# Level 64 of the first layer's cosine and sine tables: made on POOL behind its parameters, where it stood on VectorE behind the second value unit

## What is computed

```python
def hybrid_mixer(xn, ...):
    proj = xn @ w_in
    q, k, v, u_ssm, h_conv, b_gate, c_gate, gate_logits = jnp.split(proj, IN_SPLITS, axis=-1)
    y_a = stick_breaking_attention(q, k, v) @ w_br_a
    y_b = s5_ssm(u_ssm, lam_re, lam_im, log_dt, ...) @ w_br_b
    y_c = short_conv(h_conv, b_gate, c_gate, conv_w) @ w_br_c
    g = jax.nn.sigmoid(gate_logits).reshape(bsz, l, N_BRANCH, D_MODEL)
    return (g[:, :, 0] * y_a + g[:, :, 1] * y_b + g[:, :, 2] * y_c) @ w_out

def s5_ssm(u, ...):
    ab_re = exp(lr * dt) * jnp.cos(li * dt)      # per state: a decay and an angle
    ab_im = exp(lr * dt) * jnp.sin(li * dt)
    ...                                          # linear recurrence over the 256 tokens
```

## Time and profile before

| | |
|---|---|
| median of three runs | 1532.11 us (1530.73 to 1532.21) |
| the profiled execution | 1531.56 us, of which the traced span is 1529.8 us |
| PE busy | 1475.1 us (96% of the span) |
| DVE busy | 597.0 us (39%) |
| ACT busy | 345.7 us (23%) |
| POOL busy | 219.7 us (14%) |
| mean granted TensorE clock | 0.994 of full speed |

### The profile page before, as it was taken

The page is one execution under the profiler, slowest core; times in us unless marked ns, Lnnn a source line. Parts: engine busy times, 40 slices in busy tenths (PEclk is TensorE's granted clock), DMA queues, the critical chain, the costliest instruction groups (busy, mean ns, idle before and its releaser), DMA issues.

```text
span 1529.8 us, 29595 instructions
## 1 busy us (share of the span) xinstructions
PE 1475.1 (96%) x13095; PEld 910.7 (60%) x13095; DVE 597.0 (39%) x923; ACT 345.7 (23%) x424; POOL 219.7 (14%) x283
## 2 busy tenths in 40 slices
PE   7999999999999999999999999999999998999987
PEld 6988999999999988994333333333323222333221
DVE  6888667655556568564120201202012011111121
ACT  5443355434435452341000000000000000000001
POOL 3447369300000037200000000000000000000000
PEclk9999999999999999999999999999999999999998
DMA  9732394555554532489999999999999999999995
GB/s 274 238 111 83 111 285 159 202 179 180 175 193 151 174 109 83 139 320 413 411 392 419 419 419 419 418 420 419 419 420 419 420 419 420 420 419 420 418 421 227
DMA packets 146336, 464.95 MB, mean 304 GB/s; under 512 B 10144, under 2 KB 92064, under 8 KB 131872
## 3 DMA queue, kind: packets, MB, share of 16 engines
q1 hardware_dynamic: 143296, 461.40, 77.6%
q0 software_dynamic: 416, 1.05, 0.3%
q10 hardware_dynamic: 2496, 0.61, 0.3%
HBM read 461.98 MB, written 1.05 MB: 303 GB/s over the span
## 4 chain that ended last, share of the span: by engine, by line
PE 49%; DMA 10%; SPq 7%; ACT 1%; issue 1%; DVE 1%; POOL 0%; DVEq 0%; ACTq 0%; POOLq 0%
PE work L1144 11%; PE work L755 11%; PE acc L1162 10%; PE acc L1144 9%; SPq L650 7%; DMA moe_ring<-in_moe_w_down 5%; DMA moe_ring<-in_moe_w_gate 3%; PE ssm_y L1144 3%; DMA moe_ring<-in_moe_w_up 2%; PE acc L1099 1%; PE acc L1112 1%; PE work L876 0%; PE acc L755 0%; PE acc L846 0%; PE work L782 0%
## 5 line engine op out<-in xcount | busy, mean ns | idle before, releaser
L755 PE MATMUL work<-xs,parts 128*128 128x256 f32 x3600 | 455.2, 287 | 9.7 <-DVE parts L1504 4.8
L755 PEld LDWEIGHTS work<-xs,parts 128*128 128x128 f32 x3600 | 442.2, 193 | 19.8 <-issue 15.7
L1144 PE MATMUL work<-moe_ring,arena 128*32 128x448 f32 x2560 | 264.8, 540 | 7.0 <-DMA moe_ring<-in_moe_w_up 6.8
L1504 DVE TENSOR_TENSOR parts<-ring,parts 128x2048 fp32r<-128x2048 f32 x94 | 219.9, 2344 | 121.6 <-ACT parts L1238 121.4
L1162 PE MATMUL acc<-moe_ring,arena 128*32 128x512 f32 x2240 | 248.9, 594 | 18.2 <-DMA moe_ring<-in_moe_w_down 16.6
L1144 PE MATMUL acc<-moe_ring,arena 128*32 128x448 f32 x2048 | 217.2, 541 | 5.5 <-DMA moe_ring<-in_moe_w_gate 4.1
L1238 ACT ACTIVATE parts<-ring 128x2048 fp32r<-128x2048 f32 x94 | 178.9, 1908 | 89.3 <-PE work L755 62.5
L1162 PEld LDWEIGHTS acc<-moe_ring,arena 128*32 128x32 f32 x2240 | 71.2, 110 | 191.8 <-issue 147.3
L1144 PEld LDWEIGHTS work<-moe_ring,arena 128*32 128x32 f32 x2560 | 84.0, 110 | 166.4 <-issue 142.5
L1424 ACT ACTIVATE arena<-acc 128x448 f32<-128x448 f32 x32 | 15.7, 541 | 628.8 <-PE work L1144 628.8
L1911 DVE TENSOR_TENSOR arena<-arena,work 128x448 f32<-128x448 f32 x40 | 22.6, 616 | 340.4 <-ACT arena L1424 340.4
(11 more groups left out here) (312 smaller groups left out, 1057.0 us busy)
## 6 DMA issues: line engine op xcount, KB each, us to landing
moe_ring<-in_moe_w_gate SPq DMA_DIRECT2D x128, 896.0 KB, 24.4
moe_ring<-in_moe_w_up SPq DMA_DIRECT2D x128, 896.0 KB, 24.5
moe_ring<-in_moe_w_down SPq DMA_DIRECT2D x112, 1024.0 KB, 25.2
ring<-in_w_in SPq DMA_DIRECT2D x44, 1024.0 KB, 6.4
ring<-in_dense_w_gate SPq DMA_DIRECT2D x14, 1024.0 KB, 5.2
ring<-in_dense_w_up SPq DMA_DIRECT2D x14, 1024.0 KB, 4.9
ring<-in_dense_w_down SPq DMA_DIRECT2D x14, 1024.0 KB, 4.8
ring<-in_w_out SPq DMA_DIRECT2D x8, 1024.0 KB, 12.9
```

Of the source, the lines that this page charges most:

```text
L755: last = nc.tensor.matmul(out_ap, a, b, start=start and n == 0, stop=stop and n == len(pairs) - 1, skip_group_check=shared)
L1144: last = nc.tensor.matmul(banks[g][GRP * q:GRP * q + GRP, 0:CHUNK], x, w[:, q * CHUNK:q * CHUNK + CHUNK], start=k == 0, stop=k == KT - 1, ...
L1504: tt(parts[:, s % PARTS, 1, :], ring[:, n % RING, :], parts[:, s % PARTS, 0, :].bitcast(F32), ALU.subtract).then_inc(lo_ready, 1)
```

## The change

DVE keeps levels 4 to 32 and signals `level_ready` at the end of level 32. POOL waits for that behind its parameters, makes level 64 with its own `turn_table`, which it uses in layer 1 already, and a small copy behind it signals `level_made`. DVE waits for `level_made` before the first half of the last level. Layer 1 is as before.

```diff
-                link(tt(ps, p4, p4, ALU.add))
+                last = tt(ps, p4, p4, ALU.add)
+                link(last) if 4 * n < L // 2 else last.then_inc(level_ready, 1)
...
                 if not second:
+                    dve.wait_ge(level_made, 1)
                     tt(cosT[:, :, new], cosT[:, :, old], bc, ALU.mult)
...
-            TABLE_AT = [(("v", 0), 4), (("v", 0), 8), (("v", 1), 16), (("v", 1), 32), (("v", 1), 64)]
+            TABLE_AT = [(("v", 0), 4), (("v", 0), 8), (("v", 1), 16), (("v", 1), 32)]
...
                 if l:
                     for n in (4, 8, 16, 32, 64, 128):
                         turn_table(n)
+                else:
+                    pool.wait_ge(level_ready, 1)
+                    turn_table(L // 4)
+                    nc.gpsimd.tensor_copy(p2, pc).then_inc(level_made, 1)
```

More of the change, by code:

```diff
@@ L449, in trunk_kernel @@
         start_ready = sem("start_ready")
+        level_ready = sem("level_ready")
+        level_made = sem("level_made")
         last_gates = sem("last_gates")
```

## The result

| | before | after |
|---|---|---|
| median, runs beside each other | 1531.64 us (1530.15 to 1533.49, 22 runs) | 1535.02 us (1531.97 to 1536.97, 22 runs) |
| ratio | | 1.0018, 95% interval 1.0012 to 1.0024 |
| profiled execution, span | 1531.56 us, 1529.8 us | 1531.97 us, 1530.2 us |

The changed kernel is slower. Its median is 3.4 us (0.22%) higher; the ratio says 0.18%, 2.8 us, and so do the means (1534.55 less 1531.73). The profiled execution of the changed kernel is the fastest of its 22 runs and shows almost none of the loss: it is only 0.4 us above the profiled one of before. The 22 runs stand in two clumps: seven from 1531.97 to 1532.87, fifteen from 1534.69 to 1536.97, none between.

What follows compares the result with a forecast made beforehand. Before 690 us PE's stalls were taken to bound the kernel, with DMA busy behind. A gain of 1.6 us less a clock fall of 2.1 gave +0.5 on 1531.56: 1532.0 us, own range 1529.0 to 1533.4, wide range 1528.2 to 1535.2.

Steps and rivals of the forecast that it cites:

- Step 1: DVE without level 64: split of b ready at 67.2 us, PE's gap before b gone, PE 5.3 us ahead.
- Step 2: Level 64 on POOL, its products taking turns with DVE's splits: `level_made` at 78.3 us.
- Step 3: Waits for `level_made`: DVE idles some 2.7 us, and PE's tail waits 0.2 to 1.2 us for POOL's masks.
- Step 4: Convolution on DVE: `conv_ready` practically unmoved, new PE gap of 2.7 us before the branch products, gain so far 1.6 us.
- Step 5: Clock behind PE's new gap before the branch products: a fall costing 2.1 us, bounds 0 and 2.7.
- the second price: Half clock after PE's 2.75 us idling before b slowed the products of b and c, costing 2.7 us.
- (a): Clock fall behind PE's new gap before the branch products, put at 2.1 us of loss, at most 2.7.
- (b): Clock fall behind PE's old gap before b, put at 2.7 us, which the change would save.
- I take PE's lead as kept: Behind the branch products, PE's lead of 1.6 us was assumed to last; if the order is tight, all goes.
- A: Rival, faster: convolution early, PE's new gap near 1.3 us, clock holds; gain 3.8 us, 1527.8 us; chance 0.17.
- C: Rival, no gain: something other than level 64 holds the split, PE's gap before b stays; 1531.6 us; chance 0.04.
- B: Rival, slower: `level_made` at about 80.9, branch products 0.9 us late, clock falls surely; loss 3.6, 1535.2 us; chance 0.13.

Runs made afterwards that it cites:

- after_filled: Changed kernel plus 11 unread products on PE before its wait for the convolution in layer 0: 1531.59 us, ratio 0.9999; again 1531.21 us.
- before_filled: Kernel before plus 11 unread products on PE before its wait for the split of b in layer 0: 1531.25 us, ratio 0.9999; again 1530.96 us.
- after_again: Changed kernel, unedited, traced and timed a second time: ratio 1.0009 (1.0000 to 1.0018).
- dve_conv_first: Kernel before with level 64 on DVE behind c's split and both halves of the last level behind the convolution: 1533.96 us, ratio 1.0012.
- masks_first: Changed kernel with both last-level halves behind the convolution and POOL's level 64 behind the masks of softplus0: 1533.51 us, ratio 1.0014.
- conv_late_split: Changed kernel with both last-level halves behind the convolution and the split of gC's third unit behind the first scan step: 1530.16 us, ratio 0.9992.
- after_8_filled: Changed kernel plus 8 unread products on PE before its wait for the convolution in layer 0: 1531.47 us, ratio 1.0000.

## Why the prediction was wrong

**Step 1, right.** Split b runs from 65.45 to 67.80, less 0.6 that is 67.2, as said. The gap is gone, b and c are at full clock.

**Step 2, right.** POOL's six products took from 64.61 to 77.46, 12.85 us, where the turns gave 12.5 (64.0 to 76.5). `level_made` came at 79.11, less 0.6 that is 78.5, for 78.3 (the terms as written give 76.5 + 1.4 + 0.2 = 78.1). The copy and `L1647` held nothing up: two products beside them took 1.04 and 1.31. The order of the turns was as drawn: one split between products 1 and 3, 5 and 6 shut out by one split each. The Trainium skill's "SBUF — State Buffer" (Who interferes with whom) has this as a lock, held for a whole instruction by whoever issues first; the rows of 3.09, 2.97 and 3.24 us agree. The price that its GPSIMD Engine Reference (3.1) gives, an estimated 1.35 us for a product, is above what the undisturbed ones took, 1.04 and 1.31; the measurement decides, and it was right to go by layer 1's rows.

**Step 3, right.** DVE idled 2.86 us (2.7). The masks took 2.21 us and the tail waited 0.48 (0.2 to 1.2).

**Step 4, right.** `conv_ready` came at 90.69, less 0.6 that is 90.1 (89.5 to 90.7), the gap is 2.80 (2.7), and the branch products start 1.94 us before those of the first trace (1.6; 1.4 to 2.6). The masks of tail0 fell into the convolution as said.

**Step 5, wrong, and with it "the second price".** Two terms of the sum are about the clock, and both were sizes of one execution. (a) The fall behind the new gap was put at 2.1 us, with 2.7 as its bound. Against 56.6 us without a fall, the four traces give 58.10, 59.59, 59.73 and 61.07: it costs **1.5, 3.0, 3.1 and 4.5 us**. (b) The fall behind the old gap was put at 2.7 us; two of three traces have 1.5. So the branch products of before start 33.8 and 34.0 us after u in those two, not 35.1, and the lead of the changed kernel there is 0.7 to 0.8 us, not 1.94. With the mean of the traces: 57.65 for before, 59.62 for after, 2.0 us lost (against 56.6 without a fall, before is 1.1 us behind and after 3.0), where the sum had 0.5; the medians of the timed runs say 3.4, 1.3 (1532.81 beside 1531.53) and 3.4 (1534.77 beside 1531.40), their means 2.8, 1.6 and 3.1.

The bound itself was the fault more than the value. "Rows show three times" what a gap costs, but these were three places in one execution, and 2.7 was only the largest of them. Several traces of before would have shown that one gap has more than one price, 2.7 and 1.5. They would not have shown 3.0 or 4.5: so the largest price seen was no upper bound.

That the profiled execution after, 1531.97 us, meets the forecast of 1532.0 is luck: it had the shortest of the four falls, and the stage in it is 0.35 us shorter than in the first trace of before, not 0.5 longer.

**"I take PE's lead as kept", right.** From the branch products to the second tail before takes 23.3 us (58.45 - 35.11) and after_filled 23.4 (56.56 - 33.13). What was off is the lead itself, 0.7 to 0.8 us in two traces of three, by (b). And it is a lead only over a kernel before whose clock has fallen: in the filled kernels, without any fall, after is 0.4 us behind before at the second tail. The convolution is the likely reason: in after it ends 33.1 us after u, while before_filled has its branch products at 32.4 (89.75 - 57.35). That the change, its clock aside, is worth nothing, follows from step 4: `conv_ready` stays where it was, and a PE that is ahead meets it.

**The rivals.** A (faster, 1527.8 us) did not come: the gap was 2.80. C did not come. B ended at 1535.2 and the median at 1535.02, but not by its way: it had `level_made` at 80.9 and the branch products 0.9 us late, and both came early. Of it only "the clock falls surely" was right, for one gap; that its time was met is luck. The time lies outside the sum's own range (1529.0 to 1533.4 us) and inside the wide one (1528.2 to 1535.2), near its edge; the forecast of no change that can be told is wrong by the interval of 1.0012 to 1.0024. The prediction took 0.2% for the least that can be told; with 22 runs of each kernel 0.18% could.

**What stays open.** Why the fall behind the new gap lasts longer in most executions (3.4, 6.8, 10.2 and 6.8 us at half clock) than behind the old one of the same length (6.8, 3.4 and 3.4). Behind the old one stand 96 products back to back, behind the new one branch and scan products with fewer weight loads (PEld busy for 0.61 of the first stretch above); that this is the cause is argued, not shown. Nor do three traces against four prove that it is more than chance: ahead of the change, where the kernels do the same, a gap of 3.88 us has 3.4 and 6.8 us behind it too. The timed runs make a difference likely: the mean clock is 0.9950 in the 22 runs of after and 0.9958 in the 33 of before on record beside after_again.

## What to carry to other kernels

A step moved off an engine gives its time to the next thing that waits there: before it is moved, look which wait the engine's consumer meets next, and whether that end moves at all (here `conv_ready` did not, until the order on DVE was changed). A gap of PE of some 2.7 us can cost more behind it than it is long, and by another amount in each execution, so take its price from several traces, and don't take the worst of a few for a bound. And where two kernels differ by a few microseconds, look at the timed runs' spread, and at the mean clock recorded with each of them, before one trace is taken for the kernel.

## What the runs showed of the hardware

- The same instructions behind the same idle time of 2.80 us ran at half clock for 3.4, 6.8, 10.2 and 6.8 us in four executions. The fall came between 0.4 us before PE went back to work and 2.4 us after. Behind the gaps of this stage no other lengths than these three were seen in any kernel (6.8 in dve_conv_first and masks_first, 3.4 in conv_late_split).
- The length of the idling alone does not decide whether the clock falls. Near 17 us 2.53 us of it were followed by half clock in after_filled (48 products in 7.38 us) and not in after_again (6.00); one more trace shows the fall and six more show none.
- Between 60 and 120 us, idling of PE for 1.01, 1.53 and 1.69 us was not followed by a fall, 1.78 us was (conv_late_split), and so were all nine gaps of 2.64 to 3.43 us. At 287 us 2.11 us was and 2.10 was not, in two executions of one kernel. At 1450 us 2.18 us was, in dve_conv_first.
- Instructions of POOL and DVE on SBUF take turns one for one, and a chain of both can run in more than one order: the same two splits of layer 1 took 5.31 us in after_8_filled and 7.88 in both traces with five products, where PE then waited 2.1 us, 200 us behind the edit.
